# Joined down products that begin with the last block but one, residual additions ahead of the norm's scalings, and four PSUM banks for each norm's transpositions

## What is computed

```python
# first block: layer norms after each residual
h = layer_norm(ALPHA * h + 0.5 * swiglu(h, ffn1_w1, ffn1_w3, ffn1_w2), ln1_g, ln1_b)
h = layer_norm(ALPHA * h + parallel_mixer(h, ...), ln2_g, ln2_b)
h = layer_norm(ALPHA * h + memory_attention(h, mem, ...), ln3_g, ln3_b)
h = layer_norm(ALPHA * h + 0.5 * swiglu(h, ffn2_w1, ffn2_w3, ffn2_w2), ln4_g, ln4_b)
# second block, twice: RMS norms ahead of each stage
x = x + 0.5 * swiglu_ffn(rms_norm(x, ffn1_norm), ...)
x = x + mix(rms_norm(x, mix_norm)) @ w_out
x = x + 0.5 * swiglu_ffn(rms_norm(x, ffn2_norm), ...)
# after both: x = rms_norm(x, final_norm)
# third block: attention and SSD on rms_norm(x, norm1), then an expert stage on rms_norm(x, norm2)
```

## Time and profile before

| what | value |
|---|---|
| three runs | 3420.88, 3425.39, 3425.32 us |
| the profiled execution | 3426.31 us |
| its span in the trace | 3424.5 us |
| mean granted TensorE clock | 0.939 |
| TensorE busy | 3106.7 us, 91% |
| VectorE busy | 2062.9 us, 60% |
| ScalarE busy | 1341.2 us, 39% |
| DMA | 525.5 MB, 153 GB/s in the mean |

### The profile page before, as it was taken

How to read it: one execution, slowest core, us unless ns; L and a number is a source line. 1 busy time by engine, 2 the same in 40 slices (tenths; PEclk the granted TensorE clock), 3 DMA queues, 4 the chain that set the end, 5 groups by cost and what they waited for, 6 DMA issues and landing times.

```text
span 3424.5 us, 53210 instructions
## 1 busy us (share of the span) xinstructions
PE 3106.7 (91%) x19008; PEld 2738.5 (80%) x19008; DVE 2062.9 (60%) x3619; ACT 1341.2 (39%) x1953; POOL 20.8 (1%) x41
## 2 busy tenths in 40 slices
PE   8979889898999999999999899798935899999999
PEld 8967667797998798998798777785634799999998
DVE  5545452556556655557555636764499766666666
ACT  4323422334344334434334333332317744444443
POOL 0000000000000000000000000000000000000000
PEclk9989689999999999999999959898978999999999
DMA  6546134455554554554555404223410255555554
GB/s 244 186 125 216 56 127 150 139 186 180 195 184 160 183 184 167 192 187 143 176 186 181 160 28 154 99 72 119 154 62 0 86 185 186 188 188 186 184 189 154
DMA packets 141255, 525.50 MB, mean 153 GB/s; under 512 B 16154, under 2 KB 16154, under 8 KB 138320
## 3 DMA queue, kind: packets, MB, share of 16 engines
q1 hardware_dynamic: 134768, 490.79, 42.9%
q0 software_dynamic: 5520, 30.97, 2.7%
q10 hardware_dynamic: 848, 2.10, 0.2%
HBM read 520.65 MB, written 3.15 MB: 153 GB/s over the span
## 4 chain that ended last, share of the span: by engine, by line
PE 81%; DVE 12%; ACT 4%; DMA 2%; issue 2%; ACTq 0%; DVEq 0%; SPq 0%
PE psum L487 73%; PE psum L1448 2%; DMA ring<-wstream 2%; PE psum L611 1%; DVE wpair L458 1%; PE psum L1017 1%; ACT small L1819 1%; PE psum L1040 1%; DVE arena L2336 1%; PE psum L1029 1%; ACT hpair L1823 1%; DVE xpair L660 1%; PE psum L1433 0%; DVE arena L2536 0%; DVE res L849 0%
## 5 line engine op out<-in xcount | busy, mean ns | idle before, releaser
L487 PEld LDWEIGHTS psum<-xpair,wpair 128*128 128x128 f32 x11712 | 1465.2, 195 | 58.9 <-DVE wpair L458 30.1
L487 PE MATMUL psum<-xpair,wpair 128*128 128x256 f32 x11712 | 1477.9, 286 | 32.8 <-DVE wpair L458 27.2
L458 DVE TENSOR_TENSOR wpair<-ring,wpair 128x1024 fp32r<-128x1024 f32 (+1 forms) x872 | 1060.1, 1219 | 681.6 <-ACT wpair L455 679.5
L455 ACT CAST wpair<-ring 128x1024 fp32r<-128x1024 f32 (+1 forms) x872 | 908.1, 1044 | 1058.1 <-PE psum L487 918.0
L487 PE MATMUL psum<-wpair,hpair 128*128 128x512 f32 x3120 | 757.6, 392 | 13.1 <-DVE hpair L814 12.8
L487 PEld LDWEIGHTS psum<-wpair,hpair 128*128 128x128 f32 x3120 | 570.8, 189 | 122.9 <-issue 14.0
L487 PE MATMUL psum<-wpair,xpair 128*128 128x512 f32 (+3 forms) x1536 | 359.8, 396 | 27.1 <-DVE wpair L458 24.5
L487 PEld LDWEIGHTS psum<-wpair,xpair 128*128 128x128 f32 x1536 | 294.9, 198 | 91.7 <-DVE wpair L458 22.1
L791 ACT ACTIVATE small<-psum 128x256 f32<-128x256 f32 x260 | 99.9, 384 | 461.6 <-PE psum L487 461.6
L611 PE MATMUL psum<-kc,arena 128*128 128x128 f32 (+1 forms) x340 | 71.1, 366 | 159.3 <-DVEq L2546 67.3
L611 PEld LDWEIGHTS psum<-kc,arena 128*128 128x128 f32 (+1 forms) x340 | 52.9, 186 | 179.9 <-DVEq L2546 67.5
(11 more groups left out here) (303 smaller groups left out, 1609.6 us busy)
## 6 DMA issues: line engine op xcount, KB each, us to landing
ring<-wstream SPq DMA_DIRECT2D x934, 512.0 KB, 3.3
arena<-rows POOLq DMA_DIRECT2D x18, 1024.0 KB, 5.1
arena<-diag POOLq DMA_DIRECT2D x2, 1728.0 KB, 9.8
tbuf<-arena POOLq DMA_DIRECT2D x1, 2048.0 KB, 45.9
arena<-tbuf POOLq DMA_DIRECT2D x2, 1024.0 KB, 9.4
arena<-x_feat ACTq DMA_DIRECT2D x4, 256.0 KB, 8.1
res<-x_tok ACTq DMA_DIRECT2D x1, 1024.0 KB, 11.4
arena<-mem_feat POOLq DMA_DIRECT2D x1, 1024.0 KB, 5.0
```

Of the source, the lines that this page charges most:

```text
L455: eng.copy(hi, raw).then_inc(S("w_hi"), 1)
L458: eng.tensor_tensor(wpair[:, 1, o % PAIRS, 0:w], raw, hi.bitcast(F32), ALU.subtract)\
L487: mm = pe.matmul(out_, a[i], b[j], start=start and n == 0, stop=stop_ and last)
```

## The change

Six edits, one patch:

- `last_downs` makes the products of block n - 2 for t = 0 first and only then waits for the weights and the hidden block n - 1. The order of the others changes so that t = 0's banks are finished 3 and 6 matmuls after that wait.
- `dve_rms` and the written-out norms make all four residual additions before the first scaling, and both scalings of row tile 1 come ahead of all four subtractions `x_lo`.
- The subtractions go in the order 0, 2, 1, 3.
- `pe_norm` has four banks: quarters 0 and 1 in banks 6 and 7 as before, 2 and 3 in banks 0 and 2 for norms ahead of an FFN and in 4 and 5 for the others. Groups 2 and 3 wait for their scaling alone.
- At ln1 the product of line 1351, which writes bank 4, moves behind proj, and VectorE's copy of it with it.
- The waits for the row of gains stand ahead of the additions.

```diff
@@ -642,10 +642,16 @@
             return slice(4 * (i % 2), 4 * (i % 2) + 4), tt(i // 2)
+        def quarter_bank(name, i):
+
+            if i < 2:
+                return 6 + (Q[name] + i) % 2
+            return 2 * i - 4 if name in BEFORE_FFN else 2 + i
+
         def x_block(name, i, a):
             if name in NORMS:
                 f, t = quarter(i)
-                return xpair[:, a, f, t], psum[:, 6 + (Q[name] + i) % 2, :].rearrange("p (c s) -> p c s", c=4)
+                return xpair[:, a, f, t], psum[:, quarter_bank(name, i), :].rearrange("p (c s) -> p c s", c=4)
             return xpair[:, a, 2 * i:2 * i + 2, :], psum[:, 6 + (Q[name] + i) % 2, :].rearrange("p (c s) -> p c s", c=2)
         def act_x(act, name):
@@ -661,7 +667,7 @@
                .then_inc(S(f"tr_out{(Q[name] + i) % 2}"), 1)
         def dve_x(dve, name):
-            for i in range(4):
+            for i in (0, 2, 1, 3) if name in NORMS else range(4):
                 x_lo(dve, name, i)
         fresh = []
@@ -722,15 +728,14 @@
             def last_downs():
                 ws_ = []
-                for f in (n - 2, n - 1):
-                    ws_.append(weights(pe, s.slot + down_slot(f, n, per)))
-                    pe.wait_ge(S("hid_out"), f0 + f + 1)
-                for t in range(NT):
-                    for nn in range(2):
-                        for f, w in zip((n - 2, n - 1), ws_):
-                            products(pe, bank(s.tile + nn, t), [hpair[:, a, (f0 + f) % 2, tt(t)] for a in (0, 1)],
-                                     part(w, slice(nn * HALF, (nn + 1) * HALF)), False, f == n - 1,
-                                     f"lin_done{t}" if f == n - 1 else None)
+                for t, nn, j in ((0, 0, 0), (0, 1, 0), (0, 0, 1), (0, 1, 1), (1, 0, 0), (1, 0, 1), (1, 1, 0), (1, 1, 1)):
+                    f = n - 2 + j
+                    if (t, nn) == (0, 0):
+                        ws_.append(weights(pe, s.slot + down_slot(f, n, per)))
+                        pe.wait_ge(S("hid_out"), f0 + f + 1)
+                    products(pe, bank(s.tile + nn, t), [hpair[:, a, (f0 + f) % 2, tt(t)] for a in (0, 1)],
+                             part(ws_[j], slice(nn * HALF, (nn + 1) * HALF)), False, j == 1,
+                             f"lin_done{t}" if j == 1 else None)
                 for f in (n - 2, n - 1):
                     hold(s.slot + down_slot(f, n, per))
...
@@ -887,26 +893,25 @@
         def dve_rms(dve, rows, name, joint):
+            wait_row(dve, name)
             rows.add(0, 0)
             rows.add(*((0, 1) if joint else (1, 0)))
             rows.add(*((1, 0) if joint else (0, 1)))
-            wait_row(dve, name)
-            if not joint:
-                rows.add(1, 1)
+            rows.add(1, 1)
             rows.added(0)
             rows.rstd(name, 0)
             rows.rms(name, 0, 0, hn)
-            if joint:
-                rows.add(1, 1)
             rows.rms(name, 0, 1, hn)
+            dve_rms_last(dve, rows, name)
+
+        def dve_rms_last(dve, rows, name):
+
             rows.added(1)
             rows.rstd(name, 1)
             rows.rms(name, 1, 0, hn)
-            x_lo(dve, name, 0)
             rows.rms(name, 1, 1, hn)
-            x_lo(dve, name, 1)
-            x_lo(dve, name, 2)
-            x_lo(dve, name, 3)
+            for i in (0, 2, 1, 3):
+                x_lo(dve, name, i)
             rows.row_used(name)
         def dve_layer(dve, rows, name, eps, joint):
@@ -961,8 +966,19 @@
         def pe_norm(pe, name, src):
-            pe_transpose(pe, name, [[src[:, i // 2, c * P:(c + 1) * P] for c in range(4 * (i % 2), 4 * (i % 2) + 4)]
-                                    for i in range(4)], ("normed", 4 * NORMS.index(name), 1))
+            for i in range(4):
+                pe.wait_ge(S("normed"), 4 * NORMS.index(name) + i + 1)
+                q = Q[name] + i
+                if i < 2 and q >= 2:
+                    pe.wait_ge(S(f"tr_out{q % 2}"), q // 2)
+                f, t = quarter(i)
+                for j in range(4):
+                    c = f.start + j
+                    mm = pe.transpose(psum[:, quarter_bank(name, i), j * P:(j + 1) * P],
+                                      src[:, i // 2, c * P:(c + 1) * P], ident)
+                    if j == 0:
+                        release(mm)
+                mm.then_inc(S("tr_done"), 1)
         def conv(eng, chain, pad, acc, tiles, upto, taps, w0, b0=None):
@@ -1348,10 +1364,10 @@
             pe.wait_ge(S("c_rel"), 16)
             pe.wait_ge(S("c_base"), 16)
             pe_norm(pe, "ln1", res)
+            x_comes("ln1")
+
+            pe_tok(pe, "proj", xt)
             pe.matmul(psum[0:8, 4, :], relx, oneh, start=True, stop=True).then_inc(S("rel_done"), 1)
-            x_comes("ln1")
-
-            pe_tok(pe, "proj", xt)
             pe_feat(pe, "qkd", X)
             pe_tok(pe, "gate", xt)
             pe.wait_ge(S("c_normed"), 1)
@@ -1877,11 +1893,11 @@
             dve_layer(dve, rows, "ln1", LN_EPS / ALPHA ** 2, True)
             rows.row_used("ln1")
             dve_x(dve, "ln1")
+
+            lin("proj", 1, lambda n, b: copy([cq[:, 1, :], ckv[:, 1, :], vd[:, 1].rearrange("p h d -> p (h d)")][n],
+                                             b[:, 0:STAGES["proj"].widths[n]]))
             dve.wait_ge(S("rel_done"), 1)
             copy(tsb, psum[0:8, 4, :]).then_inc(S("trow"), 1)
-
-            lin("proj", 1, lambda n, b: copy([cq[:, 1, :], ckv[:, 1, :], vd[:, 1].rearrange("p h d -> p (h d)")][n],
-                                             b[:, 0:STAGES["proj"].widths[n]]))
             lin("qkd", 1, lambda n, b: copy(qkdT[:, 4 * n + 2:4 * n + 4, :].rearrange("p c s -> p (c s)"), b))
             dve.wait_ge(S("c_mixp"), 16)
             rt = rtmp.rearrange("p h a -> p (h a)")
...
```

19 lines of the change are left out of this document (4 added, 15 removed).

## The result

The changed kernel took 3388.14 us in the median of four runs (3379.55 to 3390.84) beside 3423.10 for the kernel before on the same chip: ratio 0.9894, 95% interval 0.9874 to 0.9914, 35 us less. The forecast was 3400, with a range that ended at 3391. Two more comparisons of the same pair, made for the experiments, gave 0.9905 (0.9890 to 0.9921) and 0.9887 (0.9869 to 0.9905); their medians are 35 and 42 us apart.

A forecast was written before the change was run, and what follows sets the result against it. TensorE was 81% of the chain that ended last, so only its standstill could be won. Terms summing to 25.2 us took the profiled 3426.3 to 3401.1, median forecast 3400; eight in ten: 3391 to 3411.

The forecast's parts named there:

- the passages and the end: Eleven stage changes over a norm and the peer stage's end: TensorE's waits there shorten, 24.8 us in all.
- the 5.1: At ln1: second addition 2.0 us sooner, earlier quarter 2 and line 1351 gone from there 3.1 us, together 5.1.
- 1 (the banks don't pay): At the norms: something else keeps transpositions late, leaving a gain of 7.5 us, so 3418; chance 0.07.
- 2 (a collision dearer by 8 to 11 us, or cheaper by 6): 2 MB write beside qkd and gate: dearer gives 3409, chance 0.13; cheaper gives 3394, chance 0.08.
- 4 (the change doesn't do what it says): First joined products wait as before, residual order costs 1.2 us in each of seven: near 3423; chance 0.04.
- The collision: The 2 MB write slowing the weight stream moves from proj to qkd and gate: gain 0.4 us, bounds -11 to +6.
- the turns that the Trainium skill describes: DMA queues alternate, so weight supply is the same wherever the write falls; by this alone 1.5 us, not 0.4.
- The clock: After each passage half the slow stretch is lost, 1.2 to 2.5 us, before and after alike; 3 us allowed either way.
- Rival 3: After ten restarts the clock stays at half longer; 8 us more per passage would give 3440; chance 0.03.
- The Trainium skill's rule of that rival: At the norms' transpositions: cycling through PSUM banks with small gaps between groups loses clock; trace judged against it so far.

The follow-up runs named there:

- joined products alone: Kernel before with only the new order of the joined down products: 3408.46 us, ratio 0.9959.
- move alone: Kernel before with only the small product of line 1351 and its copy moved behind proj: 3415.99 us, ratio 0.9978.
- banks and move: Kernel before with four banks, order 0, 2, 1, 3 and the moved product, but old joined products and old place of the additions: 3402.36 us, ratio 0.9941.
- additions old: Changed kernel with the fourth residual addition back between the two scalings of row tile 0 in six norms: 3389.01 us, ratio 0.9894.
- the product ahead of proj: Changed kernel with the small product and copy ahead of proj again, ln1's quarters 2 and 3 in banks 5 and 3: 3390.10 us, ratio 0.9902.
- The longer stop: Changed kernel with three more VectorE scalings ahead of the first in n2_0, n1_1 and n2_1: 3394.19 us, ratio 0.9925.
- the filled one: Changed kernel with unread products before a norm's first transposition (none in ln2) and three unread transpositions after the last: 3380.34 us, ratio 0.9879.

## Why the prediction was wrong, point by point

The gains against the second profile of the kernel before, in us by stretch:

| stretch | predicted | changed kernel, three profiles | joined products alone | move alone | banks and move | additions old |
|---|---|---|---|---|---|---|
| the passages and the end | 24.8 | 23.6, 24.1, 23.5 | 12.4 | 0.0 | 11.5 | 24.3 |
| proj to gate | 0.4 | 2.6, 2.8, 1.0 | -0.4 | 1.2 | 2.1 | 2.9 |
| gate to attention | 0 | 1.5, 1.5, 1.4 | 0.2 | 1.2 | 0.4 | 0.6 |
| attention | 0 | 7.1, 7.1, 7.1 | 0.0 | 3.2 | -2.0 | -1.9 |
| between passages, wo to norm1 | 0 | 5.4, 6.1, 5.2 | 0.2 | 0.3 | 0.9 | 3.5 |
| MoBA and SSD | 0 | 1.4, 0.2, 8.6 | 0.2 | 0.1 | -5.2 | -0.3 |
| all | 25.2 | 41.1, 40.7, 46.0 | 12.1 | 5.9 | 8.7 | 28.0 |
| at 0.50, wo to norm1 | | 47.6, 39.6, 47.8 | 66.0 | 72.6 | 57.2 | 47.8 |

(The kernel before: 72.6 us at 0.50 in that part. Start, wo, wo3 and the peer stage, between -1.1 and 1, are left out but stand in the sum.)

Two of the passages' stretches take in more than the passage. The memory attention ahead of ln3 lost 1.5 us in the changed kernel, and the stretch ahead of norm2 won 0.5. Counted from the last products ahead of each norm, the passages and the end give 24.4 to 24.9 us, and what lies between them from wo to norm1, with the memory attention, 4.0, 4.6 and 3.7 in the changed kernel, 0.2 and 1.0 for the parts alone and 2.0 with the additions old.

**The passages: right.** 7.8 for mix_0, n1_1 and mix_1 became 2.35 + 2.95 + 2.5 = 7.8. norm1 2.8 (2.8), n1_0 2.6 (2.5), ln2 2.0 (2.0), n2_0 and n2_1 0.42 each (0.35), the end 1.4 (1.4), norm2 0.8 from its last product ahead (0.5). ln1 shows 4.3 in the table and 5.0 against the first profile, on which the 5.1 was worked out. ln3 shows 0.5 and not 2.0, but its stretch takes in the memory attention, where the changed kernel has 3.4 us at 0.50 (585.5 to 588.9) that the kernel before lacks; where that stretch is missing, with the product ahead of proj and with the banks alone, it shows 2.0, and so does the passage itself in all three profiles of the changed kernel. That edits with one mechanism each could be worked out event by event from the timeline of before is the part to keep. Of the rivals, 1 (the banks don't pay) is out, since they give 11.5 us without the joined products; 2 (a collision dearer by 8 to 11 us, or cheaper by 6) and 4 (the change doesn't do what it says) are out by the rows above.

**The collision: right in kind, small in size.** 0.4 was predicted for a stretch that gave 1.0 to 2.8, with the clock behind ln1 in it: at the 84th product of proj, ahead of both places of the collision, the three profiles stood 0.6 and 0.7 ahead and 0.2 behind. From there on the gain is 2.0, 2.1 and 1.2. The write was issued where expected and the waits for weights summed to 17.7 us. By the turns that the Trainium skill describes ("DMA: Bandwidth & Descriptors", Queues, rings and completion order) the sum had been 1.5, and the traces agree with that better than with my 0.4. What I didn't ask is whether the write had to be 2 MB at all, and that, with the reads split by heads, was worth 23 us, two thirds of the whole change.

**The clock: this is the step that failed.** The prediction said that after a passage "half of that is lost, 1.2 to 2.5 us a passage, before and after alike", and allowed 3 us either way for all of the kernel. It took the stretch at 0.50 as something fixed that follows each stop. It isn't fixed. n1_1, the kernel before (stretches of 5 us, as in the earlier trace rows), and the changed one:

```profile
1352.00:1357.00 5.00, 2.58 (x13) 1.76 (x14) 4.11 (x8) 2.30 (x6) 0.00 (x0) 0.75 0.00 0
1357.00:1362.00 5.00, 4.77 (x24) 4.40 (x24) 3.75 (x4) 4.03 (x5) 0.53 (x1) 0.56 0.39 156
```

```profile
1316.00:1321.00 5.00, 3.14 (x18) 2.09 (x17) 4.08 (x8) 3.99 (x11) 0.00 (x0) 1.00 0.19 75
1321.00:1326.00 5.00, 4.17 (x34) 3.72 (x32) 4.90 (x7) 4.44 (x6) 0.53 (x1) 1.00 0.36 106
```

The clock doesn't fall at all. The same holds for n2_0 and n2_1, and in ln2, ln3 and n1_0 the stretch at 0.50 is shorter than before (3.4, 10.2 and 10.2 us for 6.8, 13.7 and 17.1). In mix_0 it is as long as before (6.8), in mix_1 in two of three profiles. A passage that TensorE leaves sooner, and in which its transpositions follow one another closely, can give back more than the time saved in it. In the profiles this doesn't come with one edit: between the passages the joined products alone give 0.2 us, the banks 1.0, all together 3.7 to 4.6 (and 2.0 with the old additions). The parts have one profile each, so this is less sure than the effect itself. The longer stop and the filled one show that effect in both directions; but as mix_0 tells, the length of the stop alone doesn't decide where the clock falls. Rival 3 had looked at the same mechanism with the wrong sign only: that more restarts would hold the clock down. The Trainium skill's rule of that rival ("TensorE: Matmul & The Clock Gate", A second HAM failure mode: psum-queue depth-cycling) isn't borne out here: the groups go through four banks with a gap of 0.21 us at 1125 to 1128, at a granted clock of 1.00, and the time at 0.50 from wo to norm1 fell from 72.6 us to 40 to 48. In mix_0 the clock fell under groups with the same gap, but it had fallen there before the change too.

**The attention: not settled.** 7.1 us of the profiles' gain lies in the 90 us from the MLA attention to the out projection, which the change doesn't touch. The engines by stretches of 10 us, the changed kernel and the one with the old additions, each from near the start of that stage:

```profile
372.00:382.00 10.00, 7.75 (x59) 7.07 (x58) 6.28 (x16) 6.02 (x25) 0.00 (x0) 1.00 0.00 0
382.00:392.00 10.00, 7.75 (x40) 6.00 (x39) 4.85 (x14) 3.32 (x12) 0.00 (x0) 0.78 0.00 0
```

```profile
373.00:383.00 10.00, 10.00 (x41) 9.07 (x40) 4.97 (x12) 3.03 (x12) 0.00 (x0) 0.50 0.00 0
383.00:393.00 10.00, 8.37 (x42) 7.81 (x42) 4.05 (x12) 4.48 (x16) 0.00 (x0) 0.67 0.00 0
```

At 1.00 TensorE does 59 matmuls in 7.75 us of work, at 0.50 41 in 10.00. These two kernels have the same instructions up to there, as has the one with the longer stops: five profiles of one program gave 86.8, 86.8, 86.8, 95.8 and 93.7 us, mean 90.0. The kernel before gave 98.6 and 94.0. With the product behind proj there are ten profiles, from 86.8 to 95.9, mean 91.0; with it ahead four, from 94.0 to 98.6, mean 95.9. That, and the 4.5 to 11 us that the move alone gave where its passages and its collision explain 1 to 3, suggests that the move helps the attention by some microseconds. By which path the traces don't show, and with draws as wide as 9 us it is no more than suggested. That it is the clock, the records of the same traces show: the changed kernel has 27.3 us at 0.50 in that stage in each of its profiles, the kernel before 49.5 and 67.9, the one with the old additions 57.9. In MoBA and SSD, where one profile of the changed kernel won 8.6 us and one 0.2, it is 107.6 us at 0.50 in that one and 128.4 and 129.6 in the others (127.2 in the kernel before). What sets it in these stages stays open.

**The sum again.** The medians gained 35, 35 and 42 us. Of that the passages and the end give 24 to 25, as predicted; proj to gate 1 to 3; the stretches between the passages 4 to 5, by the clock. The rest, 3 to 4 us in two of the comparisons and 13 in the third, is left for the attention, MoBA and SSD and the stages around them, whose clock is drawn and perhaps moved; the medians themselves can't be divided, as only one execution of each run was profiled. So the clock came to some 8 us in the first two comparisons, where the prediction allowed 3.

## What to carry to other kernels

When an edit shortens a stop of TensorE, don't price the slow stretch behind it at what it cost before: look whether the granted clock falls there at all, and let the range reach to the whole stretch's loss on the side of the gain. Stops that can't be removed can be filled with products that nobody reads; here that took away 34 us at 0.50 and a few us of time. And where a background transfer is late wherever it is put, ask first how many bytes it needs.

## What the runs showed of the hardware

- How far the granted clock repeats differs from stage to stage: two profiles of the kernel before agree within 0.15 us from the out projection to the end, while the attention stage took 86.8 to 95.8 us in five profiles of the same instructions, and MoBA and SSD 457.5 to 465.9 us in three of the changed kernel.
- A stop of 1.64 us ahead of the transpositions left the clock at 1.00 in n2_0, n1_1 and n2_1; one of 4.00 us in n2_0 brought 10.2 us at 0.50. In mix_1 the same stop of 1.64 us left it up in one profile of the changed kernel and was followed by 6.8 us at 0.50 in the two others, in mix_0 in all three.
- Transpositions are slower at the lower clock, but not by two: 8 took 1.32 us at 1.00, and 16 took 3.68 us in a stretch at 0.50, 1.4 times as long for one.
- A write of 2 MB to DRAM in rows of 2 KB took 44.7 us beside the weight stream and held the core's traffic at 121 GB/s for 30 us; the same table in 0.37 MB took 9.2 us, and the traffic of the same 30 us was 260 GB/s. Whether it is the bytes or the number of rows that costs, no run tells.
